# First expert stage of a two-block model: other time budgets for VectorE's side work, and the strews spread over one loop on GpSimd

## The reference, cut to what matters

```python
def block(hb):                                     # 128 tokens at a time
    q = (hb @ wq).reshape(tc, PEER_HEADS, 2, PEER_HALF)
    s = jnp.einsum('thpk,hpnk->thpn', q, keys)
    s_top, i_top = lax.top_k(s, PEER_TOPK)
    cand = s_top[:, :, 0, :, None] + s_top[:, :, 1, None, :]
    cid = i_top[:, :, 0, :, None] * N_KEYS + i_top[:, :, 1, None, :]
    best, pos = lax.top_k(cand.reshape(tc, PEER_HEADS, -1), PEER_TOPK)
    eid = jnp.take_along_axis(cid.reshape(tc, PEER_HEADS, -1), pos, -1)
    g = jax.nn.softmax(best.astype(jnp.float32), -1).astype(hb.dtype)
    act = jax.nn.gelu(jnp.einsum('td,thed->the', hb, u[eid]), approximate=False)
    return jnp.einsum('the,thed->td', g * act, v[eid])
```

## Time and profile before

| | us |
|---|---|
| median of 3 runs (3628.18 to 3629.72) | 3628.54 |
| profiled execution | 3628.54 |
| span of its trace | 3626.6 |
| TensorE busy in the span | 3447.6 (95%) |
| VectorE | 2641.1 (73%) |
| ScalarE | 1666.9 (46%) |
| GpSimd | 843.7 (23%) |
| strews, row gathers, value gathers on GpSimd (128 each) | 236.7, 171.1, 178.3 |

### The profile page before, as it was taken

One profiled execution on the slowest core, in us unless ns is written; L12 is line 12 of the kernel. 1 busy time (PEld: TensorE's weight loads), 2 busy tenths in 40 slices (PEclk: granted clock), 3 DMA queues, 4 the chain that ended last, 5 costly groups with the idle time before them and its releaser, 6 DMA issues. The chain is left out here.

```text
span 3626.6 us, 54805 instructions
## 1 busy us (share of the span) xinstructions
PE 3447.6 (95%) x21289; PEld 3078.7 (85%) x21289; DVE 2641.1 (73%) x5029; ACT 1666.9 (46%) x2977; POOL 843.7 (23%) x530
## 2 busy tenths in 40 slices
PE   7998999999999999998999999999997899989899
PEld 5776998999998878887778999988886889988798
DVE  4557458896896979997445984878887677667775
ACT  4344333365563333334543544843335445564554
POOL 0000007774753433331000477700000000000000
PEclk9999999999999999999999999999998999999999
DMA  5724349678998999995124778677763214532143
GB/s 220 270 96 160 126 174 320 152 198 288 372 393 309 357 371 381 387 384 196 57 88 150 224 221 233 176 266 270 268 236 153 92 70 171 190 143 99 60 186 139
DMA packets 223664, 783.57 MB, mean 216 GB/s; under 512 B 60784, under 2 KB 110448, under 8 KB 173360
## 3 DMA queue, kind: packets, MB, share of 16 engines
q1 hardware_dynamic: 149680, 645.70, 49.7%
q0 software_dynamic: 73728, 134.38, 11.8%
HBM read 721.41 MB, written 75.37 MB: 220 GB/s over the span
## 5 line engine op out<-in xcount | busy, mean ns | idle before, releaser
L3074 DVE TENSOR_TENSOR expert_ring_low<-expert_ring,expert_high 128x1024 fp32r<-128x1024 f32 x256 | 312.6, 1222 | 130.3 <-ACT expert_high L3491 123.0
L3491 ACT ACTIVATE expert_high<-expert_ring 128x1024 fp32r<-128x1024 f32 x256 | 270.4, 1056 | 275.4 <-PE ps L3425 251.3
L2013 DVE TENSOR_TENSOR expert_ring_low<-expert_ring,expert_high 128x1024 fp32r<-128x1024 f32 x256 | 311.9, 1219 | 89.0 <-ACT expert_high L2292 85.0
L2292 ACT ACTIVATE expert_high<-expert_ring 128x1024 fp32r<-128x1024 f32 x256 | 270.7, 1058 | 212.3 <-PE ps L2220 212.3
L3386 PE MATMUL ps<-hidden_high,expert_high 128*128 128x384 f32 x1024 | 352.5, 344 | 7.9 <-DVE expert_ring_low L3074 7.9
L2398 POOL DMA_INDIRECT late_pair_weights<-pair_shares,pair_spots x128 | 251.2, 1962 | 453.1 <-DVE pair_shares L1926 375.0
L3693 POOL DMA_INDIRECT pair_weights<-own_shares,own_spots x128 | 236.7, 1849 | 504.2 <-DVE own_shares L3152 437.0
L3387 PE MATMUL ps<-hidden_low,expert_high 128*128 128x384 f32 x1024 | 345.0, 337 | 0.0
L3388 PE MATMUL ps<-hidden_high,expert_ring_low 128*128 128x384 f32 x1024 | 344.7, 337 | 0.0
L2189 PE MATMUL ps<-peer_hT_high_peer,expert_high 128*128 128x256 f32 x1024 | 290.9, 284 | 5.1 <-DVE expert_ring_low L2013 5.0
L2191 PE MATMUL ps<-peer_hT_high_peer,expert_ring_low 128*128 128x256 f32 x1024 | 287.0, 280 | 0.0
(11 more groups left out here) (830 smaller groups left out, 9712.7 us busy)
## 6 DMA issues: line engine op xcount, KB each, us to landing
expert_ring<-in_peer_u SPq DMA_DIRECT2D x128, 1024.0 KB
expert_ring<-in_peer_v SPq DMA_DIRECT2D x128, 1024.0 KB
weight_ring<-in_ffn_w_up SPq DMA_DIRECT2D x22, 2048.0 KB, 7.4
weight_ring<-in_w_in SPq DMA_DIRECT2D x14, 2048.0 KB, 7.2
weight_ring<-in_w_mod SPq DMA_DIRECT2D x12, 2048.0 KB, 8.5
mod_slot<-in_w_mod SPq DMA_DIRECT2D x12, 2048.0 KB
pair_weights_in<-pair_weights SPq DMA_DIRECT2D x15, 1536.0 KB
gelu_first<-gelu_out SPq DMA_DIRECT2D x54, 384.0 KB
```

The costliest lines, as they stand in the source:

```text
L2013: dve.tensor_tensor(piece(low, n), piece(raw, n), high[:, n % LEAD, :].bitcast(F32), ALU.subtract).then_inc(low_done, 1)
L2292: act.activation(high[:, n % LEAD, :], piece(raw, n), ACT.Identity).then_inc(high_done, 1)
L3074: dve.tensor_tensor(self.piece(G.e_low, n), self.piece(G.e_raw, n), G.e_high[:, n % LEAD, :].bitcast(F32), ALU.subtract).then_inc(self.S.l ...
L3491: act.activation(G.e_high[:, n % LEAD, :], self.piece(G.e_raw, n), ACT.Identity).then_inc(S.high_done, 1)
```

## The change

Three of the four budgets change, and the strews are issued in another order: 80 ahead of the first gather instead of 96, then one in each turn of the loop from the first on (turns 0 to 47), without the sixteen in a row.

```diff
-EARLY_NS, TABLE_NS, PICKS_NS, DOWN_NS = 3200, 2200, 2450, 1550
+EARLY_NS, TABLE_NS, PICKS_NS, DOWN_NS = 3200, 3000, 2300, 1500
...
-STREWN_FIRST = 6 * PEER_TOPK
-STREWN_THEN = STREWN_FIRST + PEER_TOPK
+STREWN_FIRST = 5 * PEER_TOPK
...
-            if n == U_SLOTS - 1:
-                for m in range(STREWN_FIRST, STREWN_THEN):
-                    self.strew(pool, m)
-            if LAG <= n < LAG + PAIRS - STREWN_THEN:
-                self.strew(pool, STREWN_THEN + n - LAG)
+            if STREWN_FIRST + n < PAIRS:
+                self.strew(pool, STREWN_FIRST + n)
```

## The result

| | before | after |
|---|---|---|
| median | 3628.36 us (3626.54 to 3629.72, 4 runs) | 3654.79 us (3649.14 to 3661.55, 4 runs) |
| ratio of after to before, 95% interval | | 1.0068 (1.0053 to 1.0084) |
| profiled execution, span | 3628.54, 3626.6 us | 3655.19, 3653.3 us |

The change costs 26 us. The prediction said 3633 us within 3618 to 3646: slower, but the time lies 9 us outside its range. In the trace of the changed kernel the stage starts 1.7 us later than in that of before (gelu 0 at 494.01 against 492.34 us). Where a time of after is compared with a predicted one, these 1.7 us are taken off, and the text says "corrected".

A forecast was written before the change was run, and what follows sets the result against it. GpSimd's 5.69 us turn of row gather, value gather and strew was taken to set the loop's pace. +6.3 us at gelu 111 and -2 us after it gave +4.3 on 3628.54, so 3633 us, range 3618 to 3646.

The forecast's parts named there:

- gelu 56: ScalarE's gelu after the last exponential of the selection: starts at 785.7 us, 6.9 us late.
- the select stall: Selection work in fewer rounds makes ScalarE 6.9 us late; TensorE bears 3.2 of it, leaving +3.6 us, bounds 0 to 6.9.
- turns 3 to 9: First loop turns on GpSimd, each a row gather and a strew: 3.5 us a turn, starting at 818.3 us.
- turns 10 to 46 without their waits: GpSimd's 37 loop turns of row gather, value gather and strew: 5.69 us each, 210.5 us, with GpSimd setting the pace.
- waits for landed strews: At turns 16 and 32 GpSimd waits until all earlier strews have landed: 4 us each, 1.3 to 6.5.
- turn 47: Last loop turn with a strew: starts at 1061.3 us, its dot ending 10.7 us later and holding up ScalarE's gate step.
- gelu 111: End of the up pass's gathered rounds: 1084.0 us against 1077.74 before, so +6.3 us with the 3.6 inside it.
- gelu 111 to the end of the down pass: Fewer gathers lie ahead of the down pass's late-value hole, 59 against 61: -2 us, between 0 and -7.6.
- TensorE, 3.2 us ahead, softens the last gate: At the gate step in round 107, TensorE may be 3.2 us ahead, at 1068.9 instead of 1072.0.
- A: Rival: transfers, not GpSimd, set the loop's pace, so earlier picks save 7.3 us and the end 2: 3619 us; chance 0.22.
- B: Rival: landing waits at turns 16 and 32 cost 12 us each instead of 4: 3644 to 3649 us; chance 0.15.
- C: Rival: no change, as VectorE's lag hides the stall and loop losses equal before's: 3628.5 within 2; chance 0.13.

The follow-up runs named there:

- k11: Changed kernel without the 48 strews of its loop, those shares left out of the weight table: ratio 0.999 to the kernel before.
- k9: Changed kernel with three strews at turns 0 to 2, none in turns 3 to 9, one in each of turns 10 to 54: 3648.83 us, ratio 1.0061.
- k1: Kernel before with the three new budgets alone, its order of strews kept: 3632.84 us, ratio 1.001.
- k5: Changed kernel with each of ScalarE's gate steps one round later: 3652.22 us, ratio 1.0066 to the kernel before.
- k4: Kernel before with the last 32 strews in a row after the third row gather, none in the loop: 3621.05 us, ratio 0.9975.
- k10: Kernel before with 26 strews in a row after the third row gather and six in turns 10 to 15: 3622.25 us, ratio 0.9978.
- k8: Changed kernel with its 48 later strews in a row after the third row gather, none in the loop: 3638.07 us, ratio 1.0027.

## Why the prediction was wrong, by its own steps

| step | predicted | measured, corrected |
|---|---|---|
| gelu 56 | 785.7 | 785.6 |
| what the select stall leaves at gelu 58 | +3.6 | +6.5 |
| fourth row gather (turn 3) | 818.3 | 821.4 |
| turns 3 to 9 | 24.5 | 29.9 |
| turns 10 to 46 without their waits | 210.5 (5.69 each) | 211.8 (5.73 each) |
| waits for landed strews in them | 4 + 4 | 2.64 + 6.82 |
| waits for VectorE in them | 0 | 4.1 |
| turn 47 | 1061.3 | 1076.7 |
| gelu 111 | 1084.0 | 1102.5 |
| gelu 111 to the end of the down pass | -2 | -2.6 |

**Right.** The bound was named rightly: GpSimd's turn sets the pace from turn 10 to turn 47, and its length was read from before within 1%. So were gelu 56, the size of the two landing waits in sum (9.5 against 8 us), and the end of the stage. The idle time of GpSimd ahead of turn 3 was put at about 70 us and was 83.66, on which no term hung. The miss is 22.4 us on the profiled execution: 18.5 at gelu 111, -0.6 behind it, and 4.5 outside the stage, which no step was about; the medians, 26.4 apart, hold about the same loss.

**The failed step is the loop.** Its start, its first turns and its waits were mis-sized, by 15.4 us at turn 47 (1076.7 against 1061.3).

- 3.1 us: the loop began late, since the select stall left 6.5 and not 3.6 us. ScalarE's gelu 56 was late as forecast. I let TensorE bear 3.2 us of it, as in before. It did give back 2.1 (gelu 57 follows 2.98 us behind 56), but round 57 then took 6.90 us in place of 5.06, with TensorE never idle and its clock at 0.50 until 794.8 (the second window below).
- 5.4 us: turns 3 to 9 took 29.9 us. I priced them as GpSimd's issue alone, 3.5 each, and gave them no wait. Turn 9 waited 3.06 us for dot 6, which itself had waited 7.48 us for its row. Turn 9 also holds the first value gather, which I had put into turn 10. A row of before showed such a wait in the first turns, 3.94 us at 845.08, and I did not carry it over. In k11 the same seven turns take 24.8 us with no strew in them (822.96 to 847.74): the waits for rows and dots alone fill the time that I gave to the issue.
- 1.3 us: the turn, 5.73 in place of 5.69.
- 1.5 us: the landing waits.
- 4.1 us: three waits for VectorE in turns 15 and 16, which the forecast of an unbroken GpSimd left out.

**The second failed step is that TensorE, 3.2 us ahead, softens the last gate.** The gate that decided was the fifth, behind turn 39, not the sixth; by the forecast the two would have come to the same. Its gelu 99 came 10.9 us behind the row gather, as the 10.7 of the forecast. From there to gelu 111 twelve rounds took 59.9 us, against 60.6 at 5.05 each: 0.7 us given back, not 3.2. By way of turn 39 the 18.5 us are 15.9 (1031.7 corrected, where the forecast's own steps give 842.8 + 29 x 5.69 + 8 = 1015.8), 0.2 from there to gelu 99 and 2.5 in the twelve rounds (59.9 against 60.6 - 3.2). Why so little is given back is in six windows of after: the stall of the selection and what follows it, the hole of the first gate with what follows it, and the rounds behind the fifth gate:

```profile
774.00:788.00 14.00, 11.56 (x73) 11.24 (x71) 13.66 (x47) 7.71 (x15) 0.00 (x0) 1.00 0.43 142
788.00:794.80 6.80, 5.66 (x20) 5.69 (x21) 6.80 (x6) 5.32 (x13) 0.00 (x0) 0.50 0.73 301
832.90:846.00 13.10, 10.05 (x64) 9.73 (x62) 6.13 (x8) 3.18 (x7) 10.56 (x7) 1.00 0.94 303
846.10:856.30 10.20, 3.09 (x12) 3.12 (x13) 5.96 (x9) 5.05 (x13) 6.74 (x5) 0.50 0.82 267
1044.00:1050.80 6.80, 4.63 (x17) 4.66 (x18) 5.20 (x7) 6.15 (x15) 5.58 (x5) 0.50 0.79 236
1050.80:1084.00 33.20, 33.20 (x210) 33.20 (x210) 29.22 (x33) 18.52 (x42) 28.01 (x18) 1.00 0.97 338
```

In the first and third window, which end inside a hole, and in the last one the granted clock is 1.00, which is 2.4 GHz. In each of the three holes, before it ends, begins a stretch at 0.50, 1.2 GHz, which goes on behind it: 6.8, 10.2 and 6.8 us. In the last window TensorE is whole. In before one hole of that kind is followed by 3.4 us at 0.50 in this view:

```profile
881.90:885.30 3.40, 3.40 (x14) 3.40 (x15) 1.40 (x4) 2.42 (x6) 2.79 (x3) 0.50 1.05 396
```

Between rounds 48 and 111 such stretches add up to 30.7 us in after and 10.2 us in before. The prediction had no term for this. The difference shows as the 4.9 us by which TensorE is busy longer in the same matmuls. Not every hole is followed by such a stretch: TensorE stood from 991.8 to 994.1 us in after, and the clock stayed at 1.00. That the clock takes away what being ahead gives is read from the rows; no kernel here changed the clock by itself.

**The early gates.** The prediction let only the last gate count. For the time of gelu 111 the trace of k9 agrees: its first gate comes 5.2 us earlier than in after, its turn 47 12.6 us earlier, and its gelu 111 12.8 us earlier. It follows turn 47, not turn 10.

**The rivals.** A, that the bytes decide, fell: the loop moved 349 GB/s at a DMA share of 0.96, while k1 has 374 GB/s between 834.4 and gelu 111 and k11 381, at 1.00 and 0.99. The transfers had room, and they were asked for too late. B, the landing waits, named the side and nearly the time, 3644 to 3649 us, and not for its reason: it wanted 12 us at each, and they were 2.64 and 6.82, 1.5 us more in sum than my forecast held. Its point of decision, a wait of about 6 us, was passed by one of the two. k5 has one such wait in its loop, of 5.55 us, where after has two, and is no faster that can be measured. A loop with strews but without these waits was not tried, since two strews can add to the same place, so up to 9.5 us of the loss may be theirs. C fell with the result.

The Trainium skill (DMA: Bandwidth & Descriptors, section Anatomy of one DMA) would give a gather 3.2 us. The trace of after does not agree: the two dots above show 11.8 and 11.2 us from issue to use, inside the 9.5 to 12.2 us read from the earlier trace rows, and the measurement decides again. By that figure of the page, as an estimate, the first gate step, at 851.25, would have had its last row at 842.0 and would have waited less than half as long.

**The chances.** The range took its width from the single terms, -7.4 to +7.8 for the turn and 5 for the waits. It held no term for errors that all have one sign. Here all five parts of the 15.4 us have it, since the forecast added up issue times and waits that it knew of, and a wait that it did not know of can only add. It was close to a lower bound of the loop, taken as its middle.

## What to carry to other kernels

Work moved from an idle stretch into a loop first uses up what the issuing engine waits there, and then sets the pace. From turn 10 to 47 the 37 strews of after take 74.0 us and their gaps 11 more. GpSimd's waits for VectorE shrink from 77.4 us in k11, which has none of them, to 4.1, and with the two landing waits the turns are 29.5 us longer. In an idle stretch the same strews cost nothing that shows, as long as they end before the next gather is wanted (k4, k10, and k8 for too many). A loop time built from issue times alone is close to a lower bound: add the first turns' wait for data and the waits on other engines that the same loop shows today. And a hole in TensorE can cost twice, for the idle time and for a stretch at 1.2 GHz behind it: here 19.9 and 4.9 us.

## What was not expected of the hardware

- A stall on ScalarE in which TensorE stayed busy left the clock at 1.00. In before the gelu at 796.06 was 2.1 us late, and the clock of its window is 1.00. In after the same kind of stall, 4.7 us longer, left TensorE busy for only 11.56 of the 14 us from 774 to 788, and 6.8 us at 0.50 followed.
- A DMA share of 0.96 to 1.00 stood beside 349, 374 and 381 GB/s in after, k1 and k11. The share by itself did not tell how much more the transfers could move.
- In sum, strews and gathers took GpSimd the same time in both orders. On the page of after, the three groups:

```profile
L3692 POOL DMA_INDIRECT pair_weights<-own_shares,own_spots x128 | 236.2, 1845 | 501.9 <-DVE own_shares L3151 437.1
...
L3713 POOL DMA_INDIRECT chosen_v<-in_peer_v,spots x128 | 171.2, 1338 | 263.6 <-DVE x L3255 247.8
...
L3707 POOL DMA_INDIRECT x<-in_peer_rows,spots x128 | 169.1, 1321 | 243.6 <-DVE x L3234 213.8
```

In before they were 236.7, 178.3 and 171.1 us. Within after a strew of turns 10 to 46 took 2.00 us (73.98 us for 37), against 1.78 for the 82 ahead of 737 us. What the new order changed is above all where the strews stand.
